# First stage of a two-layer transformer kernel on one core: order of its work, its buffers, and one quarter of its first matmuls in full float32

## The chip, the core and the metric

The kernel runs on one core of a Trainium2 chip, as a single launch. Its time is device microseconds (us) from start to end; the median of three runs is 1851.11 us. The engines of a core work in parallel, each through its own list of instructions, and wait for each other on semaphores: TensorE (PE) for matrix products, VectorE (DVE) and ScalarE (ACT) for elementwise work, GpSimd (POOL), and SyncE (SP), which here issues most of the transfers from memory (DMA).

## The reference, cut to what matters

The model has two layers on 512 latent tokens and 256 context tokens of width 1024 (float32). Each layer normalises its input and modulates it by a shift and a scale that come from a small vector:

```python
mod_x = (jax.nn.silu(c) @ w_ada[l] + b_ada[l])[:, None, :]          # (1024) @ (1024 x 6144)
mod_c = (jax.nn.silu(c_ctx) @ w_ada[l] + b_ada[l])[None, None, :]
sh1x, sc1x, g1x, sh2x, sc2x, g2x = jnp.split(mod_x, 6, axis=-1)
hx = modulate(rmsnorm(x_lat, g_attn[l]), sh1x, sc1x)                # h * (1 + scale) + shift
aqx, akx, avx, bqx, bkx, bvx = split_cols(hx @ w_in[l])
```

After that come two kinds of attention, an output projection, a gated update of x, a convolutional feed-forward part and a second gated update; the same again in layer 2, and a last norm. The change touches only what lies ahead of the first `hx @ w_in[0]`: the norm of x and the first 2048 columns of `silu(c) @ w_ada[0]` (the shift and the scale of the first sub-layer), for both token streams.

## The kernel before, in words

**Split products.** TensorE multiplies values of type float32r (float32 rounded) at full rate. To keep float32 accuracy the kernel writes a matrix as a rounded part ("hi") and a rest ("lo") and adds three products: hi*hi, hi*lo, lo*hi (`three`, L1179). So each weight tile passes two steps before PE can use it: ACT rounds it (`unit_hi`, L1561, output `w_hi`) and another engine subtracts (`split_unit`, L1064 on POOL, output `w_lo`; for the first two units `first_units_lo`, L2030 on DVE). A unit is a tile of 128x1024 weights (512 KB). There are RAW = 2 raw slots and RING = 4 slots of hi and lo.

**The first stage** (all before L1182's first matmul, in `first_tiles`, L1186):

- SP (L976 to L991) issues the small tables, x (3 MB, one transfer), then four groups of modulation weights (`ada_first`, 2 MB each, each as two halves of 1 MB with a semaphore of their own); ahead of group 2 it issues weight units 0 and 1. Units 2 and 3 wait for `w_lo_done`, that is until raw slots 0 and 1 have been split; c (broadcast to all partitions), the rotary tables and two further modulation tiles are behind them in SP's order.
- Statistics of the norm: ACT squares x, one 128x768 tile of eight at a time, into two buffers (`square_x`, L1665); DVE adds them up (`add_squares`, L2048, into `sqsum`); PE sums over partitions (`first_norm_stats`, L1130, 6 matmuls, each two records); ACT takes the square root (`stats_sd`, L1568), DVE the reciprocal (`stats_scales`, L2043), PE spreads it (`first_norm_spread`, L1138).
- The modulation: a group has 512 output columns and is worked in 4 pieces of 128x1024. ACT rounds a piece into a ring of three buffers (`piece_hi`, L1591, `first_hi`), DVE subtracts (`first_pieces_lo`, L2019, `first_lo`, in place over the weights), PE multiplies: the stationary side is `silu_wide`, in which the hi and lo parts of silu(c) for both streams are four columns and the rest zero, the moving side is 512 columns of the piece; two k-tiles by two matmuls for each piece (L1489, L1491). PE then says that the piece is used, which frees its buffer. When a group is done, ACT copies its row (`copy_row`, L1600) and PE turns it into columns (`columns`, L1474).
- DVE adds the bias (`first_modulation`, L2008), forms `gs` = gain * (1 + scale) (`norm_gains`, L2037, 128x8) and then the eight tiles of `ht` = x * gs * 1/rms (L2079); ACT adds the shift and rounds (L1588, `h_hi`), DVE subtracts (L2087, `h_lo`). PE begins the first two projection tiles as soon as `h_lo` of k-tile 0 is there.

The order on each engine is written out by hand. ACT, `first_norm_hi` (L1611): group 0, the square root, group 1, units 0 and 1, group 2, rows 0 and 1, group 3, rows 2 and 3, units 2 and 3, then h. DVE, `first_norm` (L2090): all squares' sums, group 0, the reciprocal, group 1, units 0 and 1, groups 2 and 3, modulation, h. PE, `first_modulation` (L1469), after the statistics: groups 0 to 3, with the spread behind group 0 and the columns of group g-2 behind group g. POOL (L1110) splits units 2 and 3 first of all, and then follows a planned order (`mixing`). What follows the first tiles on every engine is an order from a planner, and is not touched.

Of the kernel before, what the change touches and what calls it, by code (L numbers as in the profile page):

```python
# [35 lines left out]
PIECE = 1024  # L36
PIECES = FIRST_GROUP * D // PIECE
N_PIECES = FIRST_ADA // FIRST_GROUP * PIECES
HI_RING = 3
ADA_GROUP = 2  # L40
MID_ADA, MID_END = 3 * KT, 5 * KT
ADA_PER_PAIR = [1, 2, 2]
# [533 lines left out]
def backbone(nc, x_in, cc_in, small_in, lam_in, tab_in, sel_in, first_in, ada_in, w_in, out, x_spill, c_spill):  # L576
# [20 lines left out]
    def place(name, shape, dt, offset):  # L597
        return nc.alloc_sbuf_tensor_at(name, shape, dt, offset=offset)
# [50 lines left out]
    ht = place("ht", [P, 2, TOK], f32, R_O + 6 * KB)  # L649
    ada_first = place("ada_first", [P, FIRST_ADA, D], f32, R_H)  # L650
    first_lo = place("first_lo", [P, FIRST_ADA, D], f32r, R_H)
    first_hi = place("first_hi", [P, HI_RING, PIECE], f32r, R_QKV + 36 * KB)
    silu_wide = place("silu_wide", [P, KT, P], f32r, R_QKV + 16 * KB)
    mod_row = place("mod_row", [4, FIRST_ADA * P], f32, R_QKV + 20 * KB)
    ada_b = [place(f"ada_b{i}", [P, D], f32, R_O + (14 + 4 * i) * KB) for i in range(2)]
# [62 lines left out]
    with ctx:  # L718
        ps = ctx.enter_context(nc.psum_tensor("ps", [P, 8, 512], f32))

        def sem(name):
            return ctx.enter_context(nc.semaphore(name))

        small_loaded = sem("small_loaded")
        x_loaded = sem("x_loaded")
        c_loaded = sem("c_loaded")
        c_ready = sem("c_ready")
        silu_cols_done = sem("silu_cols_done")
# [156 lines left out]
        def n_tiles(groups):  # L885
            return sum((b - a) // P for a, b in groups)
# [63 lines left out]
        def _(sp):  # L950
# [24 lines left out]

            sp.dma_start(sm[:, :], small_in).then_inc(small_loaded, 16)  # L976
            sp.dma_start(lamv[:, :, :, :].rearrange("p l a k -> p (l a k)"), lam_in).then_inc(small_loaded, 16)
            sp.dma_start(x_sb[:, :, :], x_in).then_inc(x_loaded, 16)
            n_first = FIRST_ADA // FIRST_GROUP
            for g in range(n_first):  # L980
                if g == n_first - 2:
                    for n in range(RAW):
                        load_unit(n, first=True)
                dst = ada_first[:, g * FIRST_GROUP:(g + 1) * FIRST_GROUP, :].rearrange("p a k -> p (a k)")
                for h in range(2):
                    half = slice(h * FIRST_GROUP * D // 2, (h + 1) * FIRST_GROUP * D // 2)
                    sp.dma_start(dst[:, half], first_in[g, :, half]).then_inc(first_ada_loaded[2 * g + h], 16)
            for n in range(RAW, RING):
                load_unit(n)
            load_c()  # L990
# [72 lines left out]
        def _(pool):  # L1063
# [43 lines left out]
                        nc.gpsimd.tensor_tensor(buf, buf, ri[:, r:r + 1].broadcast_to([P, k]),  # L1107
                                                ALU.mult).then_inc(scaled_done, 1)

            pool.wait_ge(w_lo_done, RAW)  # L1110
            for n in range(RAW, RING):
                split_unit(n)
            pool.wait_ge(tab_loaded, 16)
            for l in range(DEPTH):
                mixing(plans[l])
# [5 lines left out]
        def _(pe):  # L1121
# [344 lines left out]
                        if i == 0 and k == SPREAD_AT:  # L1466
                            part_spread(norm, 1)

            def first_modulation(spread):  # L1469
# [12 lines left out]
                for g in range(n_first):  # L1482
                    w = first_lo[:, g * FIRST_GROUP:(g + 1) * FIRST_GROUP, :].rearrange("p a k -> p (a k)")
                    for p in range(PIECES):
                        q = g * PIECES + p
                        pe.wait_ge(first_lo_done, q + 1)
                        for k in range(p * KT // PIECES, (p + 1) * KT // PIECES):
                            at = k * width - p * PIECE
                            nc.tensor.matmul(ps[:, g, 0:width], silu_wide[:, k, :],  # L1489
                                             first_hi[:, q % HI_RING, at:at + width], start=k == 0, stop=False)  # L1490
                            mm = nc.tensor.matmul(ps[:, g, 0:width], silu_wide[:, k, :],  # L1491
                                                  w[:, k * width:(k + 1) * width], start=False, stop=k == KT - 1)
                        mm.then_inc(first_used, 1)
                    if g == 0:
                        spread()
                    if g >= 2:
                        columns(g - 2)
                for g in range(n_first - 2, n_first):
                    columns(g)
# [57 lines left out]
        def _(act):  # L1557
# [32 lines left out]

            def piece_hi(q):  # L1591

                g, p = divmod(q, PIECES)
                act.wait_ge(first_ada_loaded[2 * g + 2 * p // PIECES], 16)
                if q >= HI_RING:
                    act.wait_ge(first_used, q - HI_RING + 1)
                w = ada_first[:, g * FIRST_GROUP:(g + 1) * FIRST_GROUP, :].rearrange("p a k -> p (a k)")
                A(first_hi[:, q % HI_RING, :], w[:, p * PIECE:(p + 1) * PIECE], ACT.Copy).then_inc(first_hi_done, 1)

            def copy_row(g):  # L1600

                act.wait_ge(first_used, (g + 1) * PIECES)
                width = FIRST_GROUP * P
                A(mod_row[:, g * width:(g + 1) * width], ps[0:4, g, 0:width], ACT.Copy).then_inc(mod_row_copied, 1)

            def first_pieces(g):

                for p in range(PIECES):
                    piece_hi(g * PIECES + p)

            def first_norm_hi():  # L1611
                first_pieces(0)
                stats_sd(("norm", 0, 0), (5, 0, 0), n_tiles(norms[0]), D)
                first_pieces(1)
                for n in range(RAW):
                    unit_hi(n)
                first_pieces(2)
                copy_row(0)
                copy_row(1)
                first_pieces(3)  # L1620
                copy_row(2)
                copy_row(3)
                for n in range(RAW, RING):
                    unit_hi(n)
                for k in range(KT):
                    for i in range(2):
                        part_hi(0, i, k)
# [34 lines left out]
            def sqrt_table():  # L1662
                A(act_scrap[:, :], sm[:, 0:1], ACT.Sqrt)
# [183 lines left out]
            sqrt_table()  # L1847
            act.wait_ge(x_loaded, 16)
            for d in range(KT):
                square_x(d, 0, 0, TOK, d)  # L1850
# [100 lines left out]
        def _(dve):  # L1951
# [67 lines left out]
            def first_pieces_lo(g):  # L2019

                for p in range(PIECES):
                    q = g * PIECES + p
# [4 lines left out]
                    V.tensor_tensor(lo, raw, first_hi[:, q % HI_RING, :].bitcast(f32), ALU.subtract) \  # L2027
                        .then_inc(first_lo_done, 1)

            def first_units_lo():  # L2030

                for c in range(RAW):
                    dve.wait_ge(w_hi_done, c + 1)
                    V.tensor_tensor(w_lo[:, c, :], w_raw[:, c, :], w_hi[:, c, :].bitcast(f32), ALU.subtract) \
                        .then_inc(w_lo_done, 1)

            def norm_gains(gs, scale_at, gain, streams=2):  # L2037
# [284 lines left out]
            for l in range(DEPTH):  # L2322
# [254 lines left out]
```

## Time and profile before

| | us |
|---|---|
| median of three runs (lowest, highest) | 1851.11 (1848.59, 1853.25) |
| the profiled execution, its own time | 1851.6 |
| its span in the trace | 1849.8 |
| PE busy in the span | 1713.6 (93%) |
| DVE, ACT, POOL busy | 1146.0, 772.9, 646.6 |
| start of the first projection matmul (L1182) | 59.57 |

Times in the trace are counted from the start of the span. In a timeline a line gives start, duration, engine, source line, operation, output<-inputs, shapes, count, and in square brackets how long the engine had been idle and what ended that.
### The profile page before, as it was taken

Reading aid. Unit: us, or ns where it says so; the run is one execution under the profiler, and the core shown is the slowest. Engines: PE = TensorE matmul, PEld = TensorE weight load, DVE = VectorE, ACT = ScalarE, POOL = GpSimd, SP = SyncE. Lnnn points to the kernel's source line nnn. Section 1 sums busy time; section 2 is a strip of 40 time slices with the busy share of each in tenths; the row PEclk is TensorE's granted clock in tenths of the full one; section 3 lists DMA queues with packets and bytes.
Section 4 is the critical chain, followed back from the end, with each engine's and each line's share of the span. In section 5 each row is a group of like instructions: output and inputs, shape, how many; then the busy total and the mean of one; then the engine's idle time right before and its main releaser. Section 6 shows DMA issues by size and latency. Waiting matters only on the chain.

```text
span 1849.8 us, 26081 instructions
## 1 busy us (share of the span) xinstructions
PE 1713.6 (93%) x9596; PEld 1440.2 (78%) x9596; DVE 1146.0 (62%) x1735; ACT 772.9 (42%) x1269; POOL 646.6 (35%) x320
## 2 busy tenths in 40 slices
PE   4799998887979999999999989999888899999997
PEld 3667876766869888888888877688776788888887
DVE  6876768667787566676435673677654765154256
ACT  6535666444234331333123333566545354243243
POOL 0354651211013233323332326464132244444442
PEclk9898999899989999999999999899999999999999
DMA  8230000023313224333433432000012123232322
GB/s 355 93 101 24 24 24 24 12 109 147 116 62 103 98 92 140 117 121 125 148 119 118 151 112 69 24 24 24 24 35 91 57 80 103 91 97 96 103 91 92
DMA packets 45430, 168.22 MB, mean 91 GB/s; under 512 B 4740, under 2 KB 6788, under 8 KB 43544
## 3 DMA queue, kind: packets, MB, share of 16 engines
q1 hardware_dynamic: 40792, 156.46, 25.3%
q10 hardware_dynamic: 4544, 10.49, 1.6%
q8 instruction: 61, 1.00, 0.2%
q14 instruction: 33, 0.27, 0.0%
HBM read 161.69 MB, written 5.24 MB: 90 GB/s over the span
## 4 chain that ended last, share of the span: by engine, by line
PE 64%; DVE 7%; issue 3%; POOL 2%; ACT 2%; DMA 0%; DVEq 0%; ACTq 0%; SPq 0%; POOLq 0%
PE ps L1182 19%; PE ps L1183 19%; PE ps L1184 19%; PE ps L1300 2%; PE ps L1314 1%; DVE sqsum L2052 1%; POOL w_lo L1067 1%; DVE junk_mid L1982 1%; DVE nb L2223 1%; PE ps L1128 1%; PE ps L1333 1%; DVE h_lo L2087 1%; PE ps L1269 1%; PE ps L1334 1%; PE ps L1388 1%
## 5 line engine op out<-in xcount | busy, mean ns | idle before, releaser
L1067 POOL TENSOR_TENSOR w_lo<-w_raw,w_hi 128x1024 fp32r<-128x1024 f32 x184 | 469.1, 2552 | 981.1 <-ACT w_hi L1566 981.0
L1182 PE MATMUL ps<-h_hi,w_hi 128*128 128x512 f32 (+1 forms) x1592 | 572.1, 359 | 17.6 <-DVE h_lo L2087 16.3
L1183 PE MATMUL ps<-h_lo,w_hi 128*128 128x512 f32 (+1 forms) x1592 | 560.7, 352 | 0.0
L1184 PE MATMUL ps<-h_hi,w_lo 128*128 128x512 f32 (+1 forms) x1592 | 559.8, 352 | 0.0
L1182 PEld LDWEIGHTS ps<-h_hi,w_hi 128*128 128x128 f32 x1592 | 306.8, 193 | 69.9 <-issue 29.2
L1184 PEld LDWEIGHTS ps<-h_hi,w_lo 128*128 128x128 f32 x1592 | 306.1, 192 | 40.1
L1183 PEld LDWEIGHTS ps<-h_lo,w_hi 128*128 128x128 f32 x1592 | 307.2, 193 | 36.1
L1566 ACT ACTIVATE w_hi<-w_raw 128x1024 fp32r<-128x1024 f32 x188 | 198.3, 1056 | 252.3 <-PE ps L1184 229.2
L1182 PE MATMUL ps<-a_hi,w_hi 128*128 128x512 f32 (+1 forms) x552 | 191.6, 347 | 1.2 <-DVE a_lo L2432 1.2
L1183 PE MATMUL ps<-a_lo,w_hi 128*128 128x512 f32 (+1 forms) x552 | 191.3, 347 | 0.0
L1184 PE MATMUL ps<-a_hi,w_lo 128*128 128x512 f32 (+1 forms) x552 | 191.0, 346 | 0.0
L2420 DVE SCALAR_TENSOR_TENSOR conv_v<-ps,sm,conv_v 128x511 f32<-128x511 f32 (+1 forms) x132 | 83.2, 658 | 141.5 <-ACT conv_v L1914 135.2
L2223 DVE TENSOR_REDUCE nb<-ps 128x1 f32<-128x768 f32 (+1 forms) x160 | 129.2, 844 | 36.4 <-PE ps L1300 36.0
L1107 POOL TENSOR_TENSOR p_sb<-p_sb,ri 128x768 f32<-128x768 f32 (+1 forms) x80 | 107.8, 1368 | 93.4 <-DVE ri L2230 93.4
L2248 DVE TENSOR_TENSOR pt_lo<-ps,pt_hi 128x512 fp32r<-128x512 f32 (+1 forms) x160 | 105.2, 673 | 56.9 <-ACT pt_hi L1775 56.1
L1764 ACT ACTIVATE p_sb<-ps,nb 128x768 f32<-128x768 f32 (+1 forms) x120 | 97.1, 813 | 75.1 <-DVE nb L2223 66.4
L2420 DVE SCALAR_TENSOR_TENSOR conv_g<-ps,sm,conv_g 128x511 f32<-128x511 f32 (+1 forms) x132 | 83.1, 658 | 69.0 <-ACT conv_g L1914 58.2
L1775 ACT ACTIVATE pt_hi<-ps 128x512 fp32r<-128x512 f32 (+1 forms) x160 | 90.6, 587 | 78.4 <-PE ps L1314 73.8
L2368 DVE SCALAR_TENSOR_TENSOR x_sb<-ps,mod,x_sb 128x512 f32<-128x512 f32 x72 | 45.4, 658 | 121.9 <-PE ps L1184 121.4
L1964 DVE CUSTOM_DVE_ANT_0 ada_junk<-ada_b,c_bc 128x1024 bf16<-128x1024 f32 x80 | 117.2, 1464 | 1.9 <-DMA ada_b<-ada_d 0.6
L1182 PEld LDWEIGHTS ps<-a_hi,w_hi 128*128 128x128 f32 x552 | 104.5, 189 | 14.8 <-DVE a_lo L2432 1.6
L1184 PEld LDWEIGHTS ps<-a_hi,w_lo 128*128 128x128 f32 x552 | 104.5, 189 | 13.0
(168 smaller groups left out, 2462.7 us busy)
## 6 DMA issues: line engine op xcount, KB each, us to landing
w_raw<-w_d SPq DMA_DIRECT2D x188, 512.0 KB, 3.5
ada_b<-ada_d SPq DMA_DIRECT2D x56, 512.0 KB, 4.3
ada_first<-first_d SPq DMA_DIRECT2D x8, 1024.0 KB, 20.9
ada_mid<-ada_d SPq DMA_DIRECT2D x16, 512.0 KB, 7.0
ada_lead<-ada_d SPq DMA_DIRECT2D x8, 512.0 KB, 3.6
x_sb<-x_d SPq DMA_DIRECT2D x1, 3072.0 KB, 11.2
x_sb<-x_d ACTq DMA_DIRECT2D x1, 3072.0 KB, 11.8
x_spill_d<-x_sb ACTq DMA_DIRECT2D x1, 2048.0 KB, 9.1
```

The source lines that it names most:

```text
L1067: nc.gpsimd.tensor_tensor(w_lo[:, c % RING, :], w_raw[:, c % RAW, :], w_hi[:, c % RING, :].bitcast(f32), ALU.subtract).then_inc(w_lo_done, 1)
L1107: nc.gpsimd.tensor_tensor(buf, buf, ri[:, r:r + 1].broadcast_to([P, k]), ALU.mult).then_inc(scaled_done, 1)
L1182: nc.tensor.matmul(out, lh, rh, start=first, stop=False)
L1183: nc.tensor.matmul(out, lh, rl_, start=False, stop=False)
L1184: return nc.tensor.matmul(out, ll, rh, start=False, stop=last)
L1566: A(w_hi[:, c % RING, :], w_raw[:, c % RAW, :], ACT.Copy).then_inc(w_hi_done, 1)
L1764: A(dst, src, ACT.Exp, bias=nb[:, sid % 8:sid % 8 + 1], accum_out=total).then_inc(exp_done, 1)
L1775: A(pt_hi[tid % TURNS][:, 0:n], ps[:, 4 + tid % TURNS, 0:n], ACT.Copy).then_inc(pt_hi_done, 1)
L1964: ins = V.tensor_tensor_reduce(junk[:, :], w, silu_c[:, s, :], 1.0, 0.0, ALU.mult, ALU.add, dst(s))
L2223: V.tensor_reduce(nb[:, sid % 8:sid % 8 + 1], src, AX.X, ALU.max, negate=True).then_inc(bias_done, 1)
L2248: V.tensor_tensor(lo[:, 0:n], ps[:, 4 + tid % TURNS, 0:n], hi[:, 0:n].bitcast(f32), ALU.subtract) \
L2420: ins = V.scalar_tensor_tensor(dst, src, sm[:, bass.ds(8 * i + w, 1)], dst, ALU.mult, ALU.add)
```

## The change: what it does

- x is loaded in two halves, with a semaphore each.
- Group 0 of the modulation is multiplied in full float32, straight from the loaded weights: 8 matmuls of 512 columns instead of 16, with no rounding and no subtraction. PE does this before the statistics of the norm.
- The ring of rounded pieces has six buffers instead of three, and holds only groups 1 to 3.
- ACT: squares, group 1, units 0 and 1, the square root, group 2, rows 0 and 1, group 3, row 2, units 2 and 3, row 3. DVE: sums, group 1, units 0 and 1, the reciprocal, groups 2 and 3, units 2 and 3, modulation. PE: group 0, statistics, group 1, the spread, groups 2 and 3.
- Units 2 and 3 are split by DVE instead of POOL, which now waits until all four are done.

```diff
-HI_RING = 3
+HI_RING = 6
...
-    first_hi = place("first_hi", [P, HI_RING, PIECE], f32r, R_QKV + 36 * KB)
+    hi_home = [R_QKV + (36 + 4 * i) * KB for i in range(HI_RING // 2)] + [R_O + (12 + 4 * i) * KB for i in range(HI_RING // 2)]
+    first_hi = [place(f"first_hi{i}", [P, PIECE], f32r, hi_home[i]) for i in range(HI_RING)]
...
-            sp.dma_start(x_sb[:, :, :], x_in).then_inc(x_loaded, 16)
...
+            sp.dma_start(x_sb[:, 0:KT // 2, :], x_in[:, 0:KT // 2, :]).then_inc(x_half_loaded, 16)
+            sp.dma_start(x_sb[:, KT // 2:KT, :], x_in[:, KT // 2:KT, :]).then_inc(x_loaded, 16)
+            load_first(0)
+            load_first(1)
+            for n in range(RAW):
+                load_unit(n, first=True)
+            for g in range(2, n_first):
+                load_first(g)
...
-            pool.wait_ge(w_lo_done, RAW)
-            for n in range(RAW, RING):
-                split_unit(n)
+            pool.wait_ge(w_lo_done, RING)
...
-                for g in range(n_first):
+                for k in range(KT):
+                    if k % (KT // 2) == 0:
+                        pe.wait_ge(first_ada_loaded[2 * k // KT], 16)
+                    w = ada_first[:, 0:FIRST_GROUP, :].rearrange("p a k -> p (a k)")
+                    mm = nc.tensor.matmul(ps[:, 0, 0:width], silu_wide[:, k, :].bitcast(f32),
+                                          w[:, k * width:(k + 1) * width], start=k == 0, stop=k == KT - 1)
+                mm.then_inc(first_used, 1)
+                first_norm_stats()
+                for g in range(1, n_first):
...
-                    if g == 0:
-                        spread()
+                    if g == 1:
+                        first_norm_spread()
...
                 if q >= HI_RING:
-                    act.wait_ge(first_used, q - HI_RING + 1)
+                    act.wait_ge(first_used, 1 + q - HI_RING + 1)
...
             def first_norm_hi():
-                first_pieces(0)
-                stats_sd(("norm", 0, 0), (5, 0, 0), n_tiles(norms[0]), D)
+                sqrt_table()
+                act.wait_ge(x_half_loaded, 16)
+                for d in range(KT):
+                    if d == KT // 2:
+                        act.wait_ge(x_loaded, 16)
+                    square_x(d, 0, 0, TOK, d)
                 first_pieces(1)
                 for n in range(RAW):
                     unit_hi(n)
+                stats_sd(("norm", 0, 0), (5, 0, 0), n_tiles(norms[0]), D)
                 first_pieces(2)
                 copy_row(0)
                 copy_row(1)
                 first_pieces(3)
                 copy_row(2)
-                copy_row(3)
                 for n in range(RAW, RING):
                     unit_hi(n)
+                copy_row(3)
...
             def first_norm():
                 s = ("norm", 0, 0)
-                first_pieces_lo(0)
+                for d in range(KT):
+                    add_squares(d, 0, TOK, d)
+                first_pieces_lo(1)
+                first_units_lo(0, RAW)
                 stats_scales(s, 0, n_tiles(norms[0]))
-                first_pieces_lo(1)
-                first_units_lo()
                 first_pieces_lo(2)
                 first_pieces_lo(3)
+                first_units_lo(RAW, RING)
                 first_modulation()
```

## Rows read from the trace of the kernel before

**Rows 1.** Table by stretches, PE: us, length, PE busy (count), PEclk, DMA share, GB/s

```profile
50.00:60.00 10.00, 1.18 (x11) 0.60 0.33 106
60.00:70.00 10.00, 10.00 (x44) 0.72 0.00 0
```

**Rows 2.** Timeline of PE, 22 to 60 us

```profile
22.02 2.69 PE L1134 MATMUL ps<-sm,sqsum 128*128 128x1 f32 x12 [22.02 <-DVE sqsum L2052]
24.57 0.77 PE L1489 MATMUL ps<-first_hi,silu_wide 128*128 128x512 f32 x1
...
28.09 0.39 PE L1489 MATMUL ps<-first_hi,silu_wide 128*128 128x512 f32 x1
28.32 0.39 PE L1491 MATMUL ps<-first_lo,silu_wide 128*128 128x512 f32 x1
...
59.57 0.77 PE L1182 MATMUL ps<-h_hi,w_hi 128*128 128x512 f32 x1 [8.73 <-DVE h_lo L2087]
```

**Rows 3.** Table by stretches again: us, length, PEclk, DMA share, GB/s

```profile
34.00:35.00 1.00, 1.00 0.04 16
```

**Rows 4.** Line L987, issues of the halves: duration ns, first and last start

```profile
L987 SPq DMA_DIRECT2D ada_first<-first_d x8: 431/444/3897, 2.1 to 11.2; - x8
```

**Rows 5.** Single issues and their us to landing: half 0, half 7, unit 3

```profile
ada_first<-first_d SPq DMA_DIRECT2D x1, 1024.0 KB, 13.2
...
ada_first<-first_d SPq DMA_DIRECT2D x1, 1024.0 KB, 24.1
...
w_raw<-w_d SPq DMA_DIRECT2D x1, 512.0 KB, 4.9
```

**Rows 6.** Timeline of DVE, 21 to 57 us

```profile
21.79 3.49 DVE L2027 TENSOR_TENSOR first_lo<-ada_first,first_hi 128x1024 fp32r<-128x1024 f32 x3
...
47.28 1.23 DVE L2027 TENSOR_TENSOR first_lo<-ada_first,first_hi 128x1024 fp32r<-128x1024 f32 x1 [0.18 <-ACT first_hi L1598]
50.88 0.17 DVE L2013 TENSOR_TENSOR mod<-ps,sm 128x16 f32<-128x16 f32 x1 [2.37 <-PE ps L1477]
...
52.26 3.88 DVE L2040 SCALAR_TENSOR_TENSOR gs<-mod,sm 128x8 f32<-128x8 f32 x2 [0.39 <-issue]
56.18 2.19 DVE L2079 SCALAR_TENSOR_TENSOR ht<-x_sb,gs,ps 128x512 f32<-128x512 f32 x4
```

**Rows 7.** Waits, 0 to 75 us: us in total, times, longest

```profile
DVE first_lo L2027 <- ACT first_hi L1598: 5.6, 6, 2.5
...
ACT first_hi L1598 <- PE ps L1491: 7.8, 5, 3.3
```

**Rows 8.** Timeline of POOL at 51 us

```profile
51.47 4.64 POOL L1067 TENSOR_TENSOR w_lo<-w_raw,w_hi 128x1024 fp32r<-128x1024 f32 x2 [51.02 <-ACT w_hi L1566]
```

**Rows 9.** Line L2040 in the whole trace: min, median, max ns

```profile
L2040 DVE SCALAR_TENSOR_TENSOR gs<-mod,sm x7: 167/168/2264, 52.3 to 1070.6; 128x8 f32<-128x8 f32 x7
```

**Rows 10.** Timeline of ACT at 13 us

```profile
12.93 2.38 ACT L1669 ACTIVATE sqt<-x_sb 128x768 f32<-128x768 f32 x3 [4.72 <-DMA x_sb<-x_d]
```

**Rows 11.** Timeline of PE's weight loads at 92 us, line L1254

```profile
92.01 0.10 PEld L1254 LDWEIGHTS ps<-a_sq,sm 128*10 128x10 f32 x2 [2.01 <-ACT a_sq L1705]
92.45 0.09 PEld L1254 LDWEIGHTS ps<-a_sq,sm 128*10 128x10 f32 x1 [0.34 <-issue]
```

**Rows 12.** Table by stretches, PE, columns as in rows 1

```profile
65.00:66.00 1.00, 1.00 (x7) 0.71 0.00 0
...
139.00:141.00 2.00, 2.00 (x4) 0.50 0.00 0
...
1376.00:1377.00 1.00, 1.00 (x6) 0.85 0.00 0
```

**Rows 13.** Timeline of PE at 137 and at 1375 us

```profile
137.62 8.04 PE L1269 MATMUL ps<-head_r,sel_rows 10*128 10x512 f32 x12
...
1374.96 1.05 PE L1314 MATMUL ps<-sm,p_sb 128*128 128x128 f32 x4
```

**Rows 14.** Groups of instructions, 0 to 75 us: busy us, mean ns

```profile
L1128 PE MATMUL ps<-sm,n_r 128*128 128x128 f32 x12 | 1.5, 274 | 0.0
L1477 PE MATMUL ps<-sm,mod_row 4*128 4x4 f32 x16 | 1.5, 202 | 0.1
```

More of the change, by code:

```diff
@@ L725, in backbone @@
         x_loaded = sem("x_loaded")
+        x_half_loaded = sem("x_half_loaded")
         c_loaded = sem("c_loaded")
@@ L977, in _, with load_first @@
             sp.dma_start(lamv[:, :, :, :].rearrange("p l a k -> p (l a k)"), lam_in).then_inc(small_loaded, 16)
-            sp.dma_start(x_sb[:, :, :], x_in).then_inc(x_loaded, 16)
             n_first = FIRST_ADA // FIRST_GROUP
-            for g in range(n_first):
-                if g == n_first - 2:
-                    for n in range(RAW):
-                        load_unit(n, first=True)
+            def load_first(g):
                 dst = ada_first[:, g * FIRST_GROUP:(g + 1) * FIRST_GROUP, :].rearrange("p a k -> p (a k)")
@@ L1467, in first_units, with first_modulation @@
                             part_spread(norm, 1)
-            def first_modulation(spread):
+            def first_modulation():
                 pe.wait_ge(silu_lo_done, 1)
@@ L1481, in first_modulation @@
                 n_first = FIRST_ADA // FIRST_GROUP
-                for g in range(n_first):
+                for k in range(KT):
[7 more added lines that the diff above has]
+                for g in range(1, n_first):
                     w = first_lo[:, g * FIRST_GROUP:(g + 1) * FIRST_GROUP, :].rearrange("p a k -> p (a k)")
                     for p in range(PIECES):
-                        q = g * PIECES + p
+                        q = (g - 1) * PIECES + p
                         pe.wait_ge(first_lo_done, q + 1)
@@ L1489, in first_modulation @@
                             nc.tensor.matmul(ps[:, g, 0:width], silu_wide[:, k, :],
-                                             first_hi[:, q % HI_RING, at:at + width], start=k == 0, stop=False)
+                                             first_hi[q % HI_RING][:, at:at + width], start=k == 0, stop=False)
                             mm = nc.tensor.matmul(ps[:, g, 0:width], silu_wide[:, k, :],
@@ L1521, in _ @@
                 if l == 0:
-                    first_norm_stats()
-                    first_modulation(first_norm_spread)
+                    first_modulation()
                 first_tiles(l)
@@ L1591, in piece_hi @@
             def piece_hi(q):
-                g, p = divmod(q, PIECES)
+                g, p = 1 + q // PIECES, q % PIECES
                 act.wait_ge(first_ada_loaded[2 * g + 2 * p // PIECES], 16)
                 if q >= HI_RING:
-                    act.wait_ge(first_used, q - HI_RING + 1)
+                    act.wait_ge(first_used, 1 + q - HI_RING + 1)
                 w = ada_first[:, g * FIRST_GROUP:(g + 1) * FIRST_GROUP, :].rearrange("p a k -> p (a k)")
-                A(first_hi[:, q % HI_RING, :], w[:, p * PIECE:(p + 1) * PIECE], ACT.Copy).then_inc(first_hi_done, 1)
+                A(first_hi[q % HI_RING][:, :], w[:, p * PIECE:(p + 1) * PIECE], ACT.Copy).then_inc(first_hi_done, 1)
             def copy_row(g):
-                act.wait_ge(first_used, (g + 1) * PIECES)
+                act.wait_ge(first_used, 1 + g * PIECES)
                 width = FIRST_GROUP * P
@@ L1608, in first_pieces @@
                 for p in range(PIECES):
-                    piece_hi(g * PIECES + p)
+                    piece_hi((g - 1) * PIECES + p)
             def first_norm_hi():
-                first_pieces(0)
-                stats_sd(("norm", 0, 0), (5, 0, 0), n_tiles(norms[0]), D)
+                sqrt_table()
[4 more added lines that the diff above has]
+                    square_x(d, 0, 0, TOK, d)
                 first_pieces(1)
@@ L1846, in _ @@
             A(lamw[:, :], lamw[:, :], ACT.Exp).then_inc(lam_exp, 1)
[L1847 to L1850, printed above, removed]
             first_norm_hi()
@@ L2021, in first_pieces_lo @@
                 for p in range(PIECES):
-                    q = g * PIECES + p
+                    q = (g - 1) * PIECES + p
                     dve.wait_ge(first_hi_done, q + 1)
@@ L2026, in first_pieces_lo, with first_units_lo @@
                                for t in (ada_first, first_lo))
-                    V.tensor_tensor(lo, raw, first_hi[:, q % HI_RING, :].bitcast(f32), ALU.subtract) \
+                    V.tensor_tensor(lo, raw, first_hi[q % HI_RING][:, :].bitcast(f32), ALU.subtract) \
                         .then_inc(first_lo_done, 1)
-            def first_units_lo():
-                for c in range(RAW):
+            def first_units_lo(a, b):
+                for c in range(a, b):
                     dve.wait_ge(w_hi_done, c + 1)
-                    V.tensor_tensor(w_lo[:, c, :], w_raw[:, c, :], w_hi[:, c, :].bitcast(f32), ALU.subtract) \
+                    V.tensor_tensor(w_lo[:, c, :], w_raw[:, c % RAW, :], w_hi[:, c, :].bitcast(f32), ALU.subtract) \
                         .then_inc(w_lo_done, 1)
@@ L2326, in _ @@
                 step(V.tensor_scalar(nlam[:, l:l + 1], nlam[:, l:l + 1], -LAM_INIT[l], None, ALU.add))
-            for d in range(KT):
-                add_squares(d, 0, TOK, d)
             first_norm()
```

## The prediction, as it was put on record

> **What bounds the kernel now.** The table by stretches shows the one poor place that the change touches: from 50 to 60 us TensorE (PE) works 1.2 of 10 us [rows 1], and its first instruction of all comes at 22.0 [rows 2]. Everything ahead of the first projection matmul (L1182, 59.57 [rows 2]) is a serial prologue, and the question is what ends last in it.
>
> The transfers first. They run until 34 us and are silent after it [rows 3]. Half 0 of the modulation weights lands at 2.1 + 13.2 = 15.3, half 7 at 11.2 + 24.1 = 35.3 [rows 4, 5]. Between the two lie 8 MB (seven halves, two units of 0.5 MB), so 2.5 us per MB: halves 1 to 3 at 17.8, 20.3, 22.8, units 0 and 1 at 24.0 and 25.3, halves 4 to 6 at 27.8, 30.3, 32.8. Then the engines. The modulation's last piece is split only at 48.5 [rows 6], 13 us after its data is there. In the waits, ScalarE (ACT) stood 7.8 us, five times, for a buffer that PE had yet to release, and VectorE (DVE) 5.6 us for ACT [rows 7]: with three buffers the stage is a loop ACT to DVE to PE and back, and no engine in it works at its own pace. At its end the two tiny `gs` operations of 128x8 take 3.88 us [rows 6], while GpSimd (POOL) splits units 2 and 3, 4.64 us from 51.47 [rows 8]; most of the same line take 0.17 us [rows 9]. They waited for POOL, and all behind them with them.
>
> **The parts of the change, on the new clock** (same landings; a piece costs ACT 0.95 us, DVE 1.14 (three in 3.49, the last 1.22 long [rows 6]), PE four matmuls 0.23 apart, 0.92 us, at 2.4 GHz and twice that at 1.2 GHz [rows 2]; ACT's 0.95 is a 1.05 us copy less what overlaps).
>
> - *x in halves.* SP issues one more transfer; its queue is far ahead, its last issue starts 24 us before it lands [rows 5]. The first half holds 1.5 of 3 MB, so I put it at 9.2 instead of 12.9. Squares and sums took from 12.93 to 22.0 [rows 2, 10]; now 9.2 to 18. Bounds: 18 if the half lands early, 22 if both land together. Either costs nothing: ACT's next work is group 1, whose data comes at 20.3, and PE is not free for the statistics before 24 (next point).
> - *Group 0 in full float32.* Out go 4 roundings, 4 subtractions and 16 matmuls; in come 8 matmuls of two passes. The nearest price is L1254, full float32 with 128 rows and 512 columns: weight loads 0.44 us apart, one for each pass, so 0.87 us a matmul at the full clock, 1.71 at half [rows 11]. PE begins at 15.3, cold. After dense work started, the pace doubled after 3.5 us once (24.57 to 28.09 [rows 2]) and after 6.0 us once (59.57 to 65.6 [rows 2, 12]). So it rises at 18.8 to 21.3, and group 0 ends at 15.3 + 7.0 + half of the cold time, 24.0 to 25.3. The statistics (2.69 us cold [rows 2], 1.35 warm) end at 26.7 at most. ACT asks for them at 26.7, behind units 0 and 1, so this is hidden; uncovered it would stop ACT and DVE 1:1, with group 2 queued behind on both.
> - *Six buffers.* ACT: pieces of group 1 at 20.3, 21.25, 22.8, 23.75; units to 26.7; the square root; group 2 at 27.8, 28.75, 30.3, 31.25. Piece q needs piece q-6 used: PE has done group 1 by 29.4, so there is no wait (with three buffers the fourth would have waited until 26.4). Copies of rows 0 and 1, then group 3 at 33.2, 34.15, 35.3, 36.25, ending 37.3. DVE: group 3's four subtractions run from 34.25 to 38.9.
> - *Units 2 and 3 on DVE, POOL's two splits gone.* Their loads are issued at 27.6 and 28.7, after DVE's units 0 and 1, and land behind half 7, about 36.5 and 37.8. ACT rounds them 37.8 to 39.7 (ahead of the copy of row 3), DVE subtracts at 38.9 and 40.05, done 41.2. That is 2.3 us more for DVE, all of it beside PE's last piece (to 40.0), ACT's copy (40.6) and PE's transposes (41.2). Bound: if unit 3 lands 4.9 us after half 7, its time in a free queue [rows 5], all ends 1.3 us later. POOL has nothing to do until the first tile is out.
> - *The end.* `mod` begins at 41.2; 1.4 us to `gs` as now (50.88 to 52.26), `gs` 0.4 instead of 3.9, so `ht` at 43.1 instead of 56.18 [rows 6].
>
> **The sum.** 56.2 - 43.1 = 13.1 us: DVE's row of subtractions goes from 26.7 us (21.8 to 48.5) to 19.6 (21.6 to 41.2), 7.1; the wait for PE's last columns from 2.4 to 0.1, 2.3; `gs` 3.5; the start 0.2. Behind `ht` I carry it over whole: DVE's and PE's work in the first tiles is unchanged, and c, the tables and the next units are loaded relative to the same events, 13 us earlier. PE idles 5 us ahead of the first tile instead of 8.7 [rows 2]; I take the same cold start there. A warm one would give back up to 2.7 us more (6.0 cold us at half pace, less the part that DVE sets).
>
> Span 1849.8 - 13.1 = 1836.7; the profiled execution adds 1.8 (1851.6), so 1838.5; the median of the runs (1851.11) is 0.5 under that execution, so **1838.0 us**. About 0.3%, 5.6 us, is what a measurement of this kernel can tell from no change.
>
> **Rivals.**
>
> *A, full float32 work does not raise the clock.* For it: L1269, also full float32, kept PE busy for 8.04 us from 137.62 [rows 13], and the granted clock stayed at 0.50, which is 1.2 GHz [rows 12]. Against it: that one fills 10 rows of the array, not 128; and at 1376 the clock rose behind a stretch in which full float32 transposes of 128 rows took 1.05 us [rows 12, 13]. Price: at the full clock PE has 7.0 + 1.35 + 1.5 (spread) + 11.0 (12 pieces) + 1.5 (columns) = 22.3 us to do from 15.3 (the two of 1.5 by [rows 14]), and ends at 37.6 plus half of the cold time. It becomes the bound (41.2) once the clock rises after 22.5. In A group 0 ends at 29.0, the statistics at 31.7, and group 1 warms the clock at 35.2 to 37.7, so PE ends at 47.6 to 48.8 and `ht` is 1.9 later: 5.5 to 6.7 us gained, 1844.4 to 1845.6. Chance 0.18.
> The Trainium skill (TensorE: Matmul & The Clock Gate, Part 4: PE-mode transpose) says that transposes don't count as PE-busy in the same way; said of the float32 passes, that is A. The rise at 1376 speaks against it here.
>
> *B, slower: the clock stays low through the whole modulation.* PE then needs nearly double its 22.3 us, to about 58.8, and `ht` starts at 60.7: 4.5 us later than now, 1855.6. By the formula of A it turns into a loss only if the clock has not risen by about 48. Against it: the same pairs of matmuls raised it at 28.09 [rows 2]. Chance 0.02.
>
> *C, the late unit 3 of above*, or another transfer as late: 1839.3 us. Chance 0.08.
>
> *D, the gain is there at `ht` but half lost behind it*, because the first tiles and their neighbours meet POOL's locks and the clock in another phase: 1844.5. Against it: the first tiles wait on engines, not on transfers (none ran from 60 to 70 [rows 1]). Chance 0.07.
>
> **The numbers.** Forecast 0.65; its own range is 1834 to 1841 (a warmer start of the first tiles, C; the three runs spread over 4.7 us). The range of 8 in 10 reaches up to A: 1834 to 1846. The bound of 0.3% is 1845.5, so A is mostly inside "faster": faster 0.88, same 0.10, slower 0.02.
>
> **What would show it.** Right: PE's first matmul near 15.3 and its clock up by 22; ACT without waits on PE; `gs` under 0.5 us; `ht` at 43. Wrong: passes of 0.85 us still at 22 to 29 and ACT's square root near 32 (A); a wait on unit 3's transfer in front of the copy of row 3 (C); `ht` at 43, but the first tile copied out later than 68 (D). A start of `ht` before 42 would mean that I have the landings wrong.

## The result, and the profile after

| | before | after |
|---|---|---|
| median (lowest, highest), 5 runs each | 1853.23 (1848.59, 1856.18) | 1841.55 (1835.05, 1842.27) |
| ratio, 95% interval | | 0.9931 [0.9909, 0.9952] |
| profiled execution, its span | 1851.6, 1849.8 | 1836.24, 1834.4 |
| `ht` starts (DVE) | 56.18 | 42.74 |
| first tile's first matmul | 59.57 | 46.13 |

The changed kernel is faster by 0.69%, 12.8 us by the ratio and 11.7 us by the two medians; the forecast was 13.1 us, from 1851.11 to 1838.0. The median is 3.55 us above 1838.0: half a microsecond above the forecast's own range (1834 to 1841), and inside the range of 8 in 10 (1834 to 1846). Of the 3.55 us, 2.12 are the kernel before, whose median over five runs is 1853.23. The changed kernel's profiled execution is 5.3 us under its own median, so the 15.4 us between the two spans overstate the gain; that trace is used for the order of events in its first stage.

DVE in the changed kernel, against [rows 6]:

```profile
10.07 0.56 DVE L2068 COPY sqsum<-sqt 128x768 f32<-128x768 f32 x1 [2.53 <-ACT sqt L1687]
10.74 7.33 DVE L2066 TENSOR_TENSOR sqsum<-sqsum,sqt 128x768 f32<-128x768 f32 x7
21.32 4.85 DVE L2041 TENSOR_TENSOR first_lo<-ada_first,first_hi 128x1024 fp32r<-128x1024 f32 x4 [3.24 <-ACT first_hi L1611]
26.09 2.35 DVE L2048 TENSOR_TENSOR w_lo<-w_raw,w_hi 128x1024 fp32r<-128x1024 f32 x2
28.36 0.18 DVE L2060 RECIPROCAL n_r<-n_sd 128x6 f32<-128x6 f32 x1
28.86 4.84 DVE L2041 TENSOR_TENSOR first_lo<-ada_first,first_hi 128x1024 fp32r<-128x1024 f32 x4 [0.32 <-ACT first_hi L1611]
34.19 4.63 DVE L2041 TENSOR_TENSOR first_lo<-ada_first,first_hi 128x1024 fp32r<-128x1024 f32 x4 [0.49 <-ACT first_hi L1611]
38.74 2.35 DVE L2048 TENSOR_TENSOR w_lo<-w_raw,w_hi 128x1024 fp32r<-128x1024 f32 x2
41.20 0.17 DVE L2027 TENSOR_TENSOR mod<-ps,sm 128x16 f32<-128x16 f32 x1
...
42.14 0.37 DVE L2054 SCALAR_TENSOR_TENSOR gs<-mod,sm 128x8 f32<-128x8 f32 x2
42.74 2.19 DVE L2093 SCALAR_TENSOR_TENSOR ht<-x_sb,gs,ps 128x512 f32<-128x512 f32 x4 [0.23 <-DVE gs L2054]
```

Units 2 and 3 are split straight behind group 3, `mod` begins 0.1 us after them, and `gs` takes 0.37 us. But DVE stands idle for 3.24 us ahead of group 1, whose data is not there before 20.2. PE, and then ACT:

```profile
15.37 9.08 PE L1492 MATMUL ps<-ada_first,silu_wide 128*128 128x512 f32 x16 [15.37 <-DMA ada_first<-first_d]
24.29 1.40 PE L1140 MATMUL ps<-sm,sqsum 128*128 128x1 f32 x12
...
46.13 0.77 PE L1188 MATMUL ps<-h_hi,w_hi 128*128 128x512 f32 x1 [4.97 <-DVE h_lo L2101]
```

```profile
24.63 1.99 ACT L1579 ACTIVATE w_hi<-w_raw 128x1024 fp32r<-128x1024 f32 x2
26.53 0.24 ACT L1589 ACTIVATE n_sd<-ps,eps 128x6 f32<-128x6 f32 x1
27.76 2.01 ACT L1611 ACTIVATE first_hi<-ada_first 128x1024 fp32r<-128x1024 f32 x2 [0.99 <-DMA ada_first<-first_d]
```

The square root (`n_sd`) follows the units without a pause, and for its pieces ACT waits only for transfers. Of the waits from 8 to 43 us, against [rows 7], none of ACT for a buffer is left:

```profile
ACT first_hi L1611 <- DMA ada_first<-first_d: 5.4, 4, 3.4
DVE first_lo L2041 <- ACT first_hi L1611: 4.1, 3, 3.2
```

### The profile page after: what moved, and what is told of

Read it like the earlier page. It is cut to its first block, busy times and chain, and to the rows that moved or that the text cites. A ratio compares the mean times of both kernels' runs of the same rounds, so it can differ in the third digit from the quotient of the medians.

```text
span 1834.4 us, 26066 instructions
## 1 busy us (share of the span) xinstructions
PE 1713.2 (93%) x9596; PEld 1437.5 (78%) x9596; DVE 1141.1 (62%) x1733; ACT 768.6 (42%) x1265; POOL 640.7 (35%) x318
## 4 chain that ended last, share of the span: by engine, by line
PE 65%; DVE 7%; issue 3%; POOL 2%; ACT 1%; DMA 0%; DVEq 0%; ACTq 0%; SPq 0%; POOLq 0%
PE ps L1188 20%; PE ps L1189 19%; PE ps L1190 19%; PE ps L1306 2%; PE ps L1320 1%; DVE sqsum L2066 1%; DVE junk_mid L1996 1%; POOL w_lo L1075 1%; PE ps L1134 1%; DVE nb L2239 1%; PE ps L1339 1%; PE ps L1394 1%; DVE h_lo L2101 1%; PE ps L1275 1%; PE ps L1340 1%
## 5 line engine op out<-in xcount | busy, mean ns | idle before, releaser
L1075 POOL TENSOR_TENSOR w_lo<-w_raw,w_hi 128x1024 fp32r<-128x1024 f32 x182 | 463.4, 2549 | 975.4 <-ACT w_hi L1579 975.2
L1188 PE MATMUL ps<-h_hi,w_hi 128*128 128x512 f32 (+1 forms) x1592 | 571.1, 359 | 14.0 <-DVE h_lo L2101 12.5
L1188 PEld LDWEIGHTS ps<-h_hi,w_hi 128*128 128x128 f32 x1592 | 306.4, 192 | 66.0 <-issue 25.3
L2239 DVE TENSOR_REDUCE nb<-ps 128x1 f32<-128x768 f32 (+1 forms) x160 | 129.3, 845 | 35.3 <-PE ps L1306 34.8
L1190 PEld LDWEIGHTS ps<-a_hi,w_lo 128*128 128x128 f32 x552 | 104.4, 189 | 13.1
## 6 DMA issues: line engine op xcount, KB each, us to landing
ada_first<-first_d SPq DMA_DIRECT2D x8, 1024.0 KB, 20.4
x_sb<-x_d ACTq DMA_DIRECT2D x1, 3072.0 KB, 11.7
```

The source lines that it names most:

```text
L1075: nc.gpsimd.tensor_tensor(w_lo[:, c % RING, :], w_raw[:, c % RAW, :], w_hi[:, c % RING, :].bitcast(f32), ALU.subtract).then_inc(w_lo_done, 1)
L1188: nc.tensor.matmul(out, lh, rh, start=first, stop=False)
L1190: return nc.tensor.matmul(out, ll, rh, start=False, stop=last)
L2239: V.tensor_reduce(nb[:, sid % 8:sid % 8 + 1], src, AX.X, ALU.max, negate=True).then_inc(bias_done, 1)
```

## The experiments

"Half 7" is the landing of the last modulation weights; it moves between executions (34.7 to 37.0 in these), so `ht` is also given behind it. Both are read from one profiled execution of each kernel. The ratio is to the kernel before as it was measured beside each (medians 1852.79 to 1854.44).

| kernel | `ht` starts, us | behind half 7, us | median us (runs) | ratio [95%] |
|---|---|---|---|---|
| before | 56.18 | 20.9 | 1853.23 (5) | |
| b_dve23 | 52.35 | 16.9 | 1849.99 (10) | 0.9978 [0.9965, 0.9992] |
| b_ring6 | 49.83 | 15.1 | 1847.19 (10) | 0.9965 [0.9954, 0.9975] |
| g0twice | 47.68 | 12.5 | 1843.99 (5) | 0.9951 [0.9934, 0.9967] |
| split_x | 46.51 | 10.7 | 1842.09 (4) | 0.9931 [0.9909, 0.9953] |
| ring3 | 45.49 | 10.6 | 1842.83 (5) | 0.9955 [0.9941, 0.9969] |
| pool23 | 44.38 | 8.6 | 1839.21 (4) | 0.9927 [0.991, 0.9943] |
| after | 42.74 | 7.5 | 1841.55 (5) | 0.9931 [0.9909, 0.9952] |
| xwhole | 42.77 | 7.6 | 1840.54 (1) | |
| g0split | 42.54 | 7.1 | 1837.55 (4) | 0.9926 [0.991, 0.9943] |
| fill_r | 44.5 | 7.5 | 1836.92 (6) | 0.991 [0.989, 0.9929] |

A straight line through the nine kernels with several runs and no fillers is time = 1792.9 + 1.08 `ht`, and the farthest off it is the changed kernel itself, 2.5 us above. So what the stage gains at `ht` arrives at the end, about one for one; and differences at `ht` under some 3 us are read in the trace, since the times don't tell them apart.

**ring3: three buffers in the changed kernel.**

```diff
-HI_RING = 6
+HI_RING = 3
...
-    hi_home = [R_QKV + (36 + 4 * i) * KB for i in range(HI_RING // 2)] + [R_O + (12 + 4 * i) * KB for i in range(HI_RING // 2)]
+    hi_home = [R_QKV + (36 + 4 * i) * KB for i in range(HI_RING)]
```

> The changed kernel with three buffers instead of six. Chain theory (the stage ends where the last landing, ACT, DVE and PE let it; a part is worth what it adds to that chain): ACT waits for PE at the fourth piece of group 1 (used at 26.5) and at most pieces after, `ht` starts at 45.5 to 46.5 instead of 42.74, time about 3 us over the changed kernel. Rival (the parts add up one by one, as in the split of the prediction's sum, where the ring was worth about 2.5 us of waits and the rest came from fewer pieces): `ht` at 45.2. Rival 2 (with group 0 gone the ring hardly matters): `ht` within 0.5 us of 42.74.

Measured: `ht` at 45.49, 3.1 us later behind the landing. Rival 2 falls. The chain theory (45.5 to 46.5) and the additive rival (45.2) lie too close together for this run to tell them apart. ACT waits for PE again:

```profile
ACT first_hi L1611 <- PE ps L1505: 4.9, 3, 2.8
```

**b_ring6: six buffers in the kernel before, nothing else.**

```diff
-HI_RING = 3
+HI_RING = 6
...
-    first_hi = place("first_hi", [P, HI_RING, PIECE], f32r, R_QKV + 36 * KB)
+    first_hi = [place(f"first_hi{i}", [P, PIECE], f32r, hi_home[i]) for i in range(HI_RING)]
```

> The kernel before with six buffers and nothing else changed. Chain theory: ACT's five waits on PE (7.8 us) go, DVE runs its 18 subtractions through from 21.8 to about 42.5, PE ends near 43, `gs` still waits for POOL, `ht` at 50 to 51 instead of 56.18, 5 to 6 us gained. Rival (the ring was not what held the stage: with more buffers the wait moves to PE's cold matmuls or to the transfers): `ht` later than 54.

Measured: `ht` at 49.83, just before the 50 to 51 expected; behind the landing it gains 5.8 us of the 13.4 of the whole change. DVE now runs through groups 2 and 3 in one piece, and what is left of the old end stands behind it:

```profile
32.52 9.32 DVE L2028 TENSOR_TENSOR first_lo<-ada_first,first_hi 128x1024 fp32r<-128x1024 f32 x8
44.54 0.17 DVE L2014 TENSOR_TENSOR mod<-ps,sm 128x16 f32<-128x16 f32 x1 [2.70 <-PE ps L1478]
...
45.93 3.87 DVE L2041 SCALAR_TENSOR_TENSOR gs<-mod,sm 128x8 f32<-128x8 f32 x2 [0.39 <-issue]
```

The wait of 2.70 for PE's columns is the one that units 2 and 3 fill in the changed kernel. GpSimd in the same run:

```profile
45.13 4.64 POOL L1068 TENSOR_TENSOR w_lo<-w_raw,w_hi 128x1024 fp32r<-128x1024 f32 x2 [44.68 <-ACT w_hi L1567]
```

It ends at 49.77, and `gs` at 49.80.

**b_dve23: in the kernel before, units 2 and 3 ahead of row 3 and split by DVE.**

```diff
-                copy_row(3)
                 for n in range(RAW, RING):
                     unit_hi(n)
+                copy_row(3)
...
-            pool.wait_ge(w_lo_done, RAW)
-            for n in range(RAW, RING):
-                split_unit(n)
+            pool.wait_ge(w_lo_done, RING)
...
                 first_pieces_lo(3)
+                first_units_lo(RAW, RING)
```

> The kernel before with units 2 and 3 rounded ahead of row 3 and split by DVE instead of POOL, nothing else. Chain theory: `gs` loses its 3.9 us and takes 0.4, DVE's two subtractions lie beside PE's last piece and the columns; `ht` at 52.5 to 53.5, 3 to 3.5 us gained. Rival (DVE's 2.3 us come on the path in place of the lock): `ht` at 55.

Measured: 4.0 us less behind the landing (`ht` at 52.35, expected 52.5 to 53.5), and `gs` short with POOL idle:

```profile
48.74 2.36 DVE L2032 TENSOR_TENSOR w_lo<-w_raw,w_hi 128x1024 fp32r<-128x1024 f32 x2 [0.20 <-ACT w_hi L1564]
51.01 0.17 DVE L2011 TENSOR_TENSOR mod<-ps,sm 128x16 f32<-128x16 f32 x1
...
51.95 0.37 DVE L2038 SCALAR_TENSOR_TENSOR gs<-mod,sm 128x8 f32<-128x8 f32 x2
```

**pool23: the opposite, POOL splits units 2 and 3 in the changed kernel.**

```diff
-            pool.wait_ge(w_lo_done, RING)
+            pool.wait_ge(w_lo_done, RAW)
+            for n in range(RAW, RING):
+                split_unit(n)
...
-                first_units_lo(RAW, RING)
```

> The changed kernel, with units 2 and 3 split by POOL again (ACT still rounds them ahead of row 3). Chain theory: POOL works from 38.7 to 43.4, DVE is free at 38.9 but the columns come at 41.2, so `mod` starts where it did; `gs` waits for POOL's lock until about 43.4, `ht` at 43.6 to 43.9, only 1 us later than 42.74. Additive rival (the lock costs 3.5 us as in the kernel before): `ht` at 46.2.

Measured: 1.1 us later behind the landing, as expected. The wait for PE's columns is back (2.38), but ACT rounds these units earlier than in the kernel before, POOL is nearly done when `gs` comes, and `gs` takes 1.55, not 3.88. The two runs do not undo and add the same thing: b_dve23 also brings ACT's rounding of the units forward, and pool23 keeps it forward. So the 4.0 us of b_dve23 are those of the two together, and no run has the rounding forward alone.

```profile
41.85 0.18 DVE L2029 TENSOR_TENSOR mod<-ps,sm 128x16 f32<-128x16 f32 x1 [2.38 <-PE ps L1485]
...
42.79 1.55 DVE L2056 SCALAR_TENSOR_TENSOR gs<-mod,sm 128x8 f32<-128x8 f32 x2
```

```profile
39.46 4.66 POOL L1075 TENSOR_TENSOR w_lo<-w_raw,w_hi 128x1024 fp32r<-128x1024 f32 x2 [39.01 <-ACT w_hi L1581]
```

**xwhole: x in one transfer. g0split: group 0 rounded, split and multiplied as the others.** Each in the changed kernel; then both together, split_x.

```diff
# xwhole
-            sp.dma_start(x_sb[:, 0:KT // 2, :], x_in[:, 0:KT // 2, :]).then_inc(x_half_loaded, 16)
-            sp.dma_start(x_sb[:, KT // 2:KT, :], x_in[:, KT // 2:KT, :]).then_inc(x_loaded, 16)
+            sp.dma_start(x_sb[:, :, :], x_in).then_inc(x_loaded, 16)
# g0split
-                for k in range(KT):
...
-                mm.then_inc(first_used, 1)
-                first_norm_stats()
-                for g in range(1, n_first):
+                for g in range(n_first):
...
+                first_pieces(0)
                 first_pieces(1)
...
+                first_pieces_lo(0)
                 first_pieces_lo(1)
```

> The changed kernel with x in one transfer. Chain theory: squares run from 12.9 to 20.6 instead of 9.1 to 16.8, ACT's first piece starts at 20.6 instead of 20.2, the statistics wait for nothing (PE is in group 0 until 24.3), `ht` at 42.7 to 43.2: worth nothing. Rival (the halves bring the norm forward, and with it the stage): `ht` 1 to 3.7 us later.

> The changed kernel with group 0 rounded and split as the others are (16 pieces, six buffers), all else of the new order kept. Chain theory: ACT idles from 16.8 to 20.2 and DVE from 18.1 to 21.3 in the changed kernel, so 3.4 and 3.2 us of the added 3.8 and 4.6 us lie in idle time; DVE then runs through from 18.1 and ends units 2 and 3 at about 41.5; `ht` at 43.2 to 44.2, 0.5 to 1.5 us later. Additive rival (four pieces at DVE's 1.14 us, as in the prediction's 7.1 us for fewer pieces and waits): `ht` at 47.3.

> The changed kernel with both of its early savings undone: group 0 rounded and split like the others, and x in one transfer. Each alone cost nothing (ht 7.1 and 7.6 us behind the landing of half 7, against 7.5). Theory (they stand in for each other: each alone leaves VectorE enough idle time ahead of the middle halves): with both gone VectorE has its sums until about 22.0, then in a row group 0 (4.6), group 1 (4.6), units 0 and 1 (2.35), groups 2 and 3 (9.3), units 2 and 3 (2.35), together 45.2, and modulation to gs 0.94 more: ht at 45.5 to 46.5, 10.5 to 11.5 behind half 7, no idle time on VectorE between 22 and 45, and 2.5 to 3.5 us more of the whole. Rival (neither does anything at ht, the six buffers and the order alone set it): ht 7 to 8 us behind half 7, as in the changed kernel, and the same time.

Measured: xwhole as expected; g0split without the loss that was expected (`mod` starts at 41.19, in the changed kernel at 41.20); split_x 3.2 us later behind the landing, as its theory says. DVE in g0split, then in split_x:

```profile
17.90 9.17 DVE L2036 TENSOR_TENSOR first_lo<-ada_first,first_hi 128x1024 fp32r<-128x1024 f32 x8
26.98 2.35 DVE L2043 TENSOR_TENSOR w_lo<-w_raw,w_hi 128x1024 fp32r<-128x1024 f32 x2
...
34.14 4.67 DVE L2036 TENSOR_TENSOR first_lo<-ada_first,first_hi 128x1024 fp32r<-128x1024 f32 x4 [0.20 <-ACT first_hi L1605]
```

```profile
22.21 9.16 DVE L2032 TENSOR_TENSOR first_lo<-ada_first,first_hi 128x1024 fp32r<-128x1024 f32 x8
31.29 2.35 DVE L2039 TENSOR_TENSOR w_lo<-w_raw,w_hi 128x1024 fp32r<-128x1024 f32 x2
33.56 0.18 DVE L2051 RECIPROCAL n_r<-n_sd 128x6 f32<-128x6 f32 x1
33.66 9.13 DVE L2032 TENSOR_TENSOR first_lo<-ada_first,first_hi 128x1024 fp32r<-128x1024 f32 x8
42.71 2.35 DVE L2039 TENSOR_TENSOR w_lo<-w_raw,w_hi 128x1024 fp32r<-128x1024 f32 x2
```

In g0split the 4.6 us of group 0 fill what was idle: 3.24, 0.32 and part of 0.49 us, and some 0.5 us inside the rows of groups 1 and 2 (4.85 and 4.84 us long, where four subtractions without a gap take 4.6). DVE still reaches group 3 at 34.14 (34.19 in the changed kernel). In split_x DVE has no pause in its row from 14.96 to 45, and its own work is the bound. So for the start of `ht` the halves of x and the full float32 are substitutes: either one is enough, the second brings nothing here, and without both 3.2 us are lost. That these 3.2 us reach the end is not shown: split_x has the same ratio as the changed kernel, with intervals of 4 us to each side.

**g0twice: every matmul of group 0 done twice in the changed kernel**, the second into a bank that nothing reads.

```diff
+                    nc.tensor.matmul(ps[:, 3, 0:width], silu_wide[:, k, :].bitcast(f32),
+                                     w[:, k * width:(k + 1) * width], start=k == 0, stop=k == KT - 1)
```

> The changed kernel with each matmul of group 0 done a second time into a bank that is cleared later: 7 us more on PE, computing nothing new. Chain theory: group 0 ends at 31.3, statistics at 32.7, ACT's square root waits until then with group 2 behind it; PE's row of work, 22.3 + 7 us at the full clock and 2 us for the cold start from 15.4, ends at 46.6 or, with the waits for group 2 behind the square root, up to 2 us later: `ht` at 48 to 51, 5.5 to 8 us later, so that PE's slack is 1.5 us at most. Rival (PE has slack before the transfers end, since it waited for DVE in groups 2 and 3): `ht` less than 3 us later.

Measured: 5.0 us later, just under the 5.5 to 8 expected and well over the rival's 3. The square root now waits 5.50 us for PE (the line below), and DVE waits 3.98 us for the square root:

```profile
32.10 0.27 ACT L1591 ACTIVATE n_sd<-ps,eps 128x6 f32<-128x6 f32 x1 [5.50 <-PE ps L1140]
```

So the cover of group 0 and the statistics is thin: the statistics end at 25.7 in the changed kernel and are asked for at 26.5. PE's first rows in this run also show the clock, each row two passes of 512 columns:

```profile
15.36 2.04 PE L1492 MATMUL ps<-ada_first,silu_wide 128*128 128x512 f32 x2 [15.36 <-DMA ada_first<-first_d]
17.20 1.62 PE L1494 MATMUL ps<-ada_first,silu_wide 128*128 128x512 f32 x2
18.66 1.02 PE L1492 MATMUL ps<-ada_first,silu_wide 128*128 128x512 f32 x2
19.52 1.02 PE L1494 MATMUL ps<-ada_first,silu_wide 128*128 128x512 f32 x2
```

1.84 us from the first to the second, 0.86 from the third to the fourth: the clock has risen by 18.7, with nothing but full float32 work on PE before it.

**fill_r, fill_f5, fill_f5r10: fillers on PE behind the last columns**, in its idle 5 us ahead of the first tile: 20 rounded matmuls, 5 in full float32, and 5 in full float32 over 10 rows. Their results are not used.

```diff
+                for k in range(20):        # fill_f5, fill_f5r10: 5, with .bitcast(f32) on both sides; fill_f5r10: rows 0:10 of both
+                    nc.tensor.matmul(ps[:, 3, 0:width], silu_wide[:, k % KT, :],
+                                     first_hi[0][:, 0:width], start=True, stop=True)
```

> The changed kernel with 20 float32r matmuls of 512 columns on PE behind the last columns (41.2), into a bank that the first tiles clear: 4.6 us of work in an idle time of 5.0, computing nothing. If idleness before the first tile is what lowers the clock there: the clock is still at 1.00 at 46, the first tile starts within 0.3 us of 46.1, the 4.0 cold us go, and the first tiles end 1.2 to 2 us earlier (ACT's silu of c at 58 instead of 59.66). Rival (it fell for another reason, or DVE's pace sets the first tiles): no change, or PE's late start costs 0.5 us.

> The changed kernel with 5 filler matmuls in full float32, 128 rows and 512 columns, on PE behind the last columns, 4.4 us of work ahead of the first tile; their result is not used. Theory (full float32 holds the clock as rounded work does): granted clock 1.00 in the stretches 42:44 to 46:48, where the changed kernel shows 0.50, and the first tile's matmuls start at full pace (0.23 us apart), first copy to a_raw 20 to 21 us behind ht instead of 22.2. Rival (it does not count as busy): granted clock down to 0.50 by 46, the fillers' passes 0.85 us apart at the end, and the first tile cold.

> As the run with 5 full float32 fillers, but each fills only 10 rows of the array (the contraction has 10 partitions) and still streams 512 columns. Theory (what L1269 in the trace of before suggests: PE busy for 8 us with 10 rows and no rise of the clock): granted clock falls to 0.50 by 46 as in the changed kernel with an idle PE, the passes go from 0.43 to 0.85 us apart, the first tile is cold. Rival (rows do not matter, the cause at L1269 was another): clock 1.00 through 42 to 48, as with 128 rows.

Measured, in rows of the table by stretches. The first is the changed kernel without fillers (us, length, then busy us of PE, PEld, DVE, ACT and POOL, PEclk, DMA share, GB/s):

```profile
44.00:46.00 2.00, 0.00 (x0) 0.00 (x0) 2.00 (x5) 1.69 (x4) 0.00 (x0) 0.50 0.82 326
```

Then fill_f5, and behind it fill_f5r10 (us, length, PE busy, PEclk, DMA share, GB/s):

```profile
44.00:46.00 2.00, 2.00 (x6) 1.00 0.96 385
46.00:48.00 2.00, 1.52 (x5) 1.00 0.14 53
```

```profile
44.00:46.00 2.00, 2.00 (x3) 0.50 0.99 397
46.00:48.00 2.00, 2.00 (x4) 0.50 0.23 90
```

With 128 rows the clock stays at 2.4 GHz (in fill_r too) and the first tile starts at full pace; with 10 rows PE is just as busy, and the clock falls to 1.2 GHz, as it does in the changed kernel with PE idle. The fillers' ten passes took 4.56 us in one run and 7.48 in the other.

What the warm start is worth: ACT's first copy of a tile (`a_raw`) comes 20.4 us after `ht` in fill_r and in fill_f5 instead of 22.2. But ACT's root for the heads of the first tiles (`head_r`) comes 69.0 and 68.8 us after `ht`, in the changed kernel 68.5, so that the 1.8 us are gone by then. The traces show where a part of them goes. At 76 us PE waits for ACT's squares of the heads (`a_sq`). In the changed kernel it waits 1.58 us and the clock stays at 1.00 in every stretch from 72 to 88. In fill_r it waits 2.28 us (in fill_f5 2.09), the clock falls behind that, and the next four passes take 2.25 us (2.46) instead of 1.46. PE in the changed kernel, then in fill_r, and fill_r's stretch:

```profile
77.62 1.46 PE L1260 MATMUL ps<-a_sq,sm 128*10 128x512 f32 x4 [1.58 <-ACT a_sq L1723]
```

```profile
78.29 2.25 PE L1260 MATMUL ps<-a_sq,sm 128*10 128x512 f32 x4 [2.28 <-ACT a_sq L1726]
```

```profile
80.00:82.00 2.00, 2.00 (x6) 0.50 0.04 4
```

What was won at the cold start is in part paid again in a second one.

Silu of c starts 16.92 us after `ht` with and without fillers, so this mark of fill_r's expectation did not move. fill_r's time is the lowest in the table, but its interval overlaps the changed kernel's; no better kernel is shown. fill_f5 and fill_f5r10 ran once each: 1840.36 and 1843.45 us.

## Why the prediction was right, point by point

- **The landings, and with them the pace from 20 us on:** half 7 was put at 35.3 and came at 35.2; x's first half at 9.2, and came at 9.1; units 2 and 3 were loaded in time, since ACT rounds them at 37.62 without a wait (C fell). "Silent after 34" holds only for the microsecond of [rows 3]: in the kernel before the next loads are issued at 36.1, and the share of the DMA engines is 0.47 from 35 to 40 us and 0.75 from 40 to 50. In the changed kernel they are issued at 27.3 and follow half 7 directly (0.98 from 38 to 40).
- **Group 0 in full float32:** expected from 15.3 to between 24.0 and 25.3, measured 15.37 to 24.3. The clock rose during it, so rival A fell. The row that spoke for A [rows 12, 13] fills 10 rows of the array, and fill_f5 and fill_f5r10, which differ in nothing but that number, agree with it: 1.00 against 0.50 from 44 to 48 us. The Trainium skill (TensorE: Matmul & The Clock Gate, Part 4: PE-mode transpose) says of transposes that they don't count as PE-busy in the same way; carried over to these float32 passes of 128 rows, it does not hold. The row at 1376, which the prediction set against A, is weaker than it was made: between 1373.5 and 1376.2 PE did rounded matmuls as well as transposes.
- **DVE's row of subtractions** 19.8 us (19.6 predicted), **the wait for the columns** 0.1, **`gs`** 0.37, and 0.94 instead of 1.38 us from `mod` to `gs`, a term that was carried over unchanged: the 0.39 us "issue" ahead of `gs` is gone, in pool23 too, and no run shows why. Together `ht` at 42.74 against 43.1, 13.4 us earlier instead of 13.1.
- **Carried over behind `ht`:** right to within 2 us (D, which would lose 6.5, fell; the first tile is copied out at 64.92, not later than 68). From `ht` to the end of the span it was 1793.6 us and is 1791.7 in the profiled executions; over the other kernels without fillers it is 1792.8 to 1796.0. The medians differ by 11.7 us where `ht` moved by 13.4, so by them 1.8 us are lost on the way. The two signs disagree, the difference is within the spread of the runs (7 us), and the slope of 1.08 says one for one.
- **B** fell with the clock: it had risen by 18.7.

What the sum did not say, and the runs do: the shares don't belong to the parts one by one. Six buffers are worth 5.8 us alone and 3.1 as the last part added; the splits taken off POOL 1.1 last, and 4.0 alone together with ACT's earlier rounding; full float32 and the halves of x nothing last, 3.2 together. The place of the square root behind units 0 and 1 was undone in no run. The prediction booked the 7.1 us of DVE's row as one sum and never asked which part would be missed. It said rightly that halves of x cost and gain nothing while group 0 is off DVE, but not that the same holds the other way round. The expectation of g0split (0.5 to 1.5 us of loss) counted the 3.2 us of idle time ahead of group 1, and missed the smaller pauses ahead of groups 2 and 3 and inside their rows.

PE's slack has two bounds in the prediction. The one on PE's whole work (41.2 once the clock rises after 22.5) was made for a late clock. The other, that uncovered statistics stop ACT and DVE 1:1, is the one that g0twice meets first: group 0 ends 6.4 us later, the cover was 0.8, the square root comes 5.6 later and `ht` 5.0.

## What to carry to other kernels

When a prologue is fed by transfers, work out the distance from the last landing to its end, and count only what shortens that; everything ahead of the last landings is worth something only as far as an engine has no idle time there, and two parts that remove the same wait can't both be paid for. Judge parts by undoing each in the new kernel and by adding each to the old one, with the same edit both ways: for the six buffers the two values are 3.1 and 5.8 us, and the difference is what they share with the other parts. Before giving work to another engine, look at what the tiny operations behind it do meanwhile.

## What the runs showed of the hardware that was not expected

- `gs` is two 128x8 operations of 0.17 us each. In the kernel before, each of them ended 0.03 us after the POOL operation that was under way when it started. DVE, then POOL:

```profile
52.26 1.58 DVE L2040 SCALAR_TENSOR_TENSOR gs<-mod,sm 128x8 f32<-128x8 f32 x1 [0.39 <-issue]
53.88 2.26 DVE L2040 SCALAR_TENSOR_TENSOR gs<-mod,sm 128x8 f32<-128x8 f32 x1
```

```profile
51.47 2.34 POOL L1067 TENSOR_TENSOR w_lo<-w_raw,w_hi 128x1024 fp32r<-128x1024 f32 x1 [51.02 <-ACT w_hi L1566]
53.78 2.33 POOL L1067 TENSOR_TENSOR w_lo<-w_raw,w_hi 128x1024 fp32r<-128x1024 f32 x1
```

The second ended in the same way in b_ring6 (49.80 against 49.77). In pool23 the first ended 0.02 us after POOL's second split and the other ran freely behind it. With POOL idle the two took 0.37 in all ten kernels of that kind. The additions of `mod`, which read PSUM, took 0.17 or 0.18 us beside POOL (four in pool23). So a small DVE operation can be held up for the whole rest of a POOL operation, and not every one is.
- Ten rows against 128 (fill_f5r10, fill_f5, one execution each): the same instructions and columns, PE busy from 44 to 46 in both, and the granted clock 0.50 against 1.00.
- A wait of PE of 2.28 and of 2.09 us near 76 was followed by a clock of 0.50 from 80 to 82 (fill_r) and of 0.54 from 78 to 80 (fill_f5); one of 1.58 us at the same place was not (the changed kernel).
- From an idle PE the clock rose 4.0 us after the first tile's start (46.13 to 50.10) where it took 5.9 before (59.57 to 65.47), and about 3.3 us after 15.36 in full float32 (g0twice).
